# Down-projection weight loads issued by ScalarE on its own DMA queue, in a mixture-of-experts block

## The reference

```python
x = x + merged @ w_out[l]                       # attention and pooling, 256 x 1024
h2 = rms_norm(x, norm2_g[l])
x = x + moe_ffn(h2, router_w[l], ...)

def moe_ffn(...):                               # top 4 of 32 experts, softmax gates
    ...
    def run_block(args):
        tok, e = args
        xb = h_pad[tok]
        gu = xb @ w_gate_up[e] + b_gate_up[e]                  # 1024 x 2048
        gate = jnp.minimum(gu[:, :EXPERT_DIM], SWIGLU_LIMIT)
        up = jnp.clip(gu[:, EXPERT_DIM:], -SWIGLU_LIMIT, SWIGLU_LIMIT)
        act = gate * jax.nn.sigmoid(SWIGLU_ALPHA * gate) * (up + 1.0)
        return act @ w_down[e] + b_down[e]                     # 1024 x 1024
```

## Time and profile before

| | us |
|---|---|
| median of 3 runs | 1127.81 |
| lowest and highest | 1127.17, 1128.42 |
| the profiled execution | 1124.1 |
| its span | 1122.3 |

### The profile page before, as it was taken

How to read it: one execution, slowest core, us unless ns; L and a number is a source line. 1 busy time by engine, 2 the same in 40 slices (tenths; PEclk the granted TensorE clock), 3 DMA queues, 4 the chain that set the end, 5 groups by cost and what they waited for, 6 DMA issues and landing times.

```text
span 1122.3 us, 11997 instructions
## 1 busy us (share of the span) xinstructions
PE 1051.0 (94%) x4830; PEld 439.1 (39%) x4830; DVE 290.4 (26%) x592; ACT 118.0 (11%) x210; POOL 7.7 (1%) x16
## 2 busy tenths in 40 slices
PE   7999999999999999999999989898989899999988
PEld 4444545543434343434343424242424243333332
DVE  2654032332222222221212121221212212212221
ACT  3124101201000000000000000000000000000001
POOL 2000000000000000000000000000000000000000
PEclk9999999999999999999999999999999999999999
DMA  9932573899999999999999999999999999999995
GB/s 335 392 130 84 216 279 117 336 385 430 428 427 428 429 425 427 422 429 429 428 428 427 430 429 429 429 428 429 427 430 429 429 428 428 430 426 430 429 429 220
DMA packets 40256, 430.32 MB, mean 383 GB/s; under 512 B 5024, under 2 KB 5152, under 8 KB 15536
## 3 DMA queue, kind: packets, MB, share of 16 engines
q1 hardware_dynamic: 39280, 428.11, 91.4%
q0 software_dynamic: 672, 1.91, 0.5%
q10 hardware_dynamic: 288, 0.08, 0.0%
HBM read 429.03 MB, written 1.05 MB: 383 GB/s over the span
## 4 chain that ended last, share of the span: by engine, by line
PE 73%; DMA 22%; DVE 2%; issue 1%; ACT 0%; SPq 0%; DVEq 0%
PE bank L1194 28%; DMA slot<-w_gate_up_dram 18%; PE bank L1219 14%; PE bank L917 9%; PE bank L1139 5%; PE bank L1168 5%; DMA slot<-w_down_dram 4%; PE bank L941 4%; PE bank L1208 2%; DVE x L838 2%; PE bank L1117 1%; PE bank L892 1%; PE bank L1179 1%; DMA consts<-consts_dram 0%; PE bank L1235 0%
## 5 line engine op out<-in xcount | busy, mean ns | idle before, releaser
L1194 PE MATMUL bank<-slot,scr 128*64 128x512 f32 x2048 | 458.8, 596 | 20.5 <-DMA slot<-w_gate_up_dram 20.4
L1194 PEld LDWEIGHTS bank<-slot,scr 128*64 128x64 f32 x2048 | 142.3, 137 | 305.9 <-issue 268.6
L1219 PE MATMUL bank<-slot,scr 128*64 128x512 f32 x1008 | 229.1, 596 | 11.1 <-DMA slot<-w_down_dram 10.4
L813 DVE COPY scr<-bank 128x512 f32<-128x512 f32 x32 | 22.1, 691 | 456.6 <-PE bank L1194 456.6
L1219 PEld LDWEIGHTS bank<-slot,scr 128*64 128x64 f32 x1008 | 68.6, 137 | 144.9 <-issue 120.0
L917 PE MATMUL bank<-slot,scr 128*128 128x512 f32 (+1 forms) x256 | 103.3, 563 | 0.8 <-DVE scr L531 0.8
L1168 PE MATMUL bank<-scr 64*128 64x512 f32 x240 | 59.6, 613 | 22.0 <-DVE x L838 22.0
L838 DVE TENSOR_TENSOR x<-bank,x 128x512 f32<-128x512 f32 x64 | 41.4, 686 | 105.3 <-PE bank L1168 103.1
L819 DVE TENSOR_TENSOR scr<-bank,bgu 128x512 f32<-128x512 f32 x64 | 41.2, 686 | 104.9 <-PE bank L1208 104.9
L917 PEld LDWEIGHTS bank<-slot,scr 128*128 128x128 f32 x256 | 46.5, 194 | 53.7 <-issue 52.5
L1139 PEld LDWEIGHTS bank<-scr,xn 128*128 128x128 f32 x480 | 57.7, 196 | 12.2 <-issue 12.2
(11 more groups left out here) (184 smaller groups left out, 389.1 us busy)
## 6 DMA issues: line engine op xcount, KB each, us to landing
slot<-w_gate_up_dram SPq DMA_DIRECT2D x128, 2048.0 KB, 29.2
slot<-w_down_dram SPq DMA_DIRECT2D x63, 2048.0 KB, 20.9
slot<-w_in_dram SPq DMA_DIRECT2D x14, 1024.0 KB, 15.5
slot<-w_out_dram SPq DMA_DIRECT2D x4, 1024.0 KB, 4.9
slot<-w_branch_attn_dram SPq DMA_DIRECT2D x2, 1024.0 KB, 13.9
slot<-w_branch_pool_dram SPq DMA_DIRECT2D x2, 1024.0 KB, 8.5
slot<-w_down_dram SPq DMA_DIRECT2D x2, 1024.0 KB, 7.2
x<-x_dram SPq DMA_DIRECT2D x2, 512.0 KB, 5.7
```

What stands on the lines that cost most here:

```text
L813: V.tensor_copy(gu_sb[:, 512:1024], GB[1][:, :]).then_inc(gu_copied[1], 1)
L1194: ins = MM(GB[h][T * g:T * g + T, :], xgT[:, k, T * e:T * e + T], gu_slot[s][:, c0:c0 + 512], start=k == 0, stop=k == KC - 1)
L1219: ins = MM(DB[T * h:T * h + T, :], actT[e][:, c, :], v3(dn_slot[j][:, :], 4)[:, k, 512 * h:512 * h + 512], start=c == 0, stop=c == KC - 1)
```

## The change

SP's program loses the down loads of the loop and their waits (`downs_a`, `downs_b`). It issues gate/up loads alone, each as soon as its slot is used; the loops for the first pairs become one plain loop. The first two down loads (expert 0) and the last two (expert 31) stay on SP. ScalarE issues the others: after each `copy_d` it issues the two down units of the next expert, on its own queue. It needs no wait of its own for the slots, since `copy_d` waited for `dn_used[1]` and so for both halves. Sizes, slots and all other engines' programs are as before.

```diff
-            gates_a(2, 1)
-            gates_b(2, 1)
-            downs_b(0, 2)
-            for p in range(2, EARLY):
-                ahead = EARLY - p
-                gates_a(2 * p, p, 0, ahead)
-                downs_a(2 * p - 2, 2 * p - 1)
-                gates_a(2 * p, p, ahead, 4)
-                gates_b(2 * p, p, 0, ahead)
-                downs_b(2 * p - 2, 2 * p)
-                gates_b(2 * p, p, ahead, 4)
+            for p in range(1, EARLY):
+                gates_a(2 * p, p)
+                gates_b(2 * p, p)
...
-            downs_a(2 * EARLY - 2, 2 * EARLY - 1)
             with sp.Fori(EARLY - 1, n - 1) as it:
...
                 gates_a(here, q)
-                downs_b(sp.snap(2 * (it % PAIRS)), q2)
                 gates_b(here, q)
-                downs_a(here, q3)
...
+            def load_down(expert):
+                for j in range(DN_SLOTS):
+                    act.dma_start(dn_slot[j][:, :], dn_src(expert, j)).then_inc(dn_in[j], 16)
+
+            def pair(here, after, q, q1, q2, q3, last):
                 act.wait_ge(done["S"], q)
                 nc.scalar.activation(selgT, SB[:, :], ACT.Copy).then_inc(read["S"], 1)
                 copy_gu(1, q, q2)
                 sigmoid(q2)
                 copy_d(0, q2)
                 if not last:
+                    load_down(here + 1)
+                if not last:
                     copy_gu(0, q1, q3)
                     sigmoid(q3)
                     copy_d(1, q3)
+                    load_down(after)
```

More of the change, by code:

```diff
@@ L308, in gates_b @@
                     load_gu(4 + i, expert + 1)
[L310 to L318, removed]
-            gates_a(2, 1)
-            gates_b(2, 1)
-            downs_b(0, 2)
-            for p in range(2, EARLY):
-                ahead = EARLY - p
-                gates_a(2 * p, p, 0, ahead)
-                downs_a(2 * p - 2, 2 * p - 1)
-                gates_a(2 * p, p, ahead, 4)
-                gates_b(2 * p, p, 0, ahead)
-                downs_b(2 * p - 2, 2 * p)
-                gates_b(2 * p, p, ahead, 4)
+            for p in range(1, EARLY):
+                gates_a(2 * p, p)
+                gates_b(2 * p, p)
             sp.wait_ge(n_ready, 1)
             n = sp.value_load(n_t[0:1, 0:1], min_val=PAIRS, max_val=4 * PAIRS)
-            downs_a(2 * EARLY - 2, 2 * EARLY - 1)
             with sp.Fori(EARLY - 1, n - 1) as it:
-                here, q, q2, q3 = sp.snap(2 * ((it + 1) % PAIRS)), sp.snap(it + 1), sp.snap(2 * it + 2), sp.snap(2 * it + 3)
+                here, q = sp.snap(2 * ((it + 1) % PAIRS)), sp.snap(it + 1)
                 gates_a(here, q)
-                downs_b(sp.snap(2 * (it % PAIRS)), q2)
                 gates_b(here, q)
-                downs_a(here, q3)
             sp.wait_ge(dn_used[0], sp.snap(2 * n))
@@ L481, in copy_d @@
                 nc.scalar.activation(dsb[:, 512 * e:512 * e + 512], DB[:, :], ACT.Copy).then_inc(d_copied, 1)
-            def pair(q, q1, q2, q3, last):
+            def load_down(expert):
+                for j in range(DN_SLOTS):
+                    act.dma_start(dn_slot[j][:, :], dn_src(expert, j)).then_inc(dn_in[j], 16)
+            def pair(here, after, q, q1, q2, q3, last):
                 act.wait_ge(done["S"], q)
@@ L492, in pair @@
                     copy_d(1, q3)
+                    load_down(after)
             copy_gu(0, 1, 1)
             sigmoid(1)
-            pair(1, 2, 2, 3, False)
+            pair(0, 2, 1, 2, 2, 3, False)
             act.wait_ge(n_ready, 1)
@@ L499, in _ @@
             with act.Fori(1, n - 1) as it:
-                pair(act.snap(it + 1), act.snap(it + 2), act.snap(2 * it + 2), act.snap(2 * it + 3), False)
-            pair(n, None, act.snap(2 * n), act.snap(2 * n + 1), True)
+                pair(act.snap(2 * (it % PAIRS)), act.snap(2 * ((it + 1) % PAIRS)), act.snap(it + 1), act.snap(it + 2), act.snap(2 * it + 2), act.snap(2 * it + 3), False)
+            pair(None, None, n, None, act.snap(2 * n), act.snap(2 * n + 1), True)
             act.wait_ge(d_done, act.snap(2 * n + 1))
```

## The result

| | before | after |
|---|---|---|
| median, us | 1127.17 | 1146.03 |
| lowest and highest | 1123.89, 1128.42 | 1145.82, 1151.41 |
| runs | 5 | 5 |
| profiled execution | 1124.1 | 1146.0 |
| its span | 1122.3 | 1144.2 |

The changed kernel takes 1.0182 times as long (95% interval 1.0162 to 1.0202), 18.9 us by the medians. The forecast was 1151.1, with 1137 to 1160 as its range. The profiled executions lie 21.9 us apart; the forecast for that pair was 23.3.

The account below looks back on a forecast made before the run. DMA engines bound the late stage (58.7 us a pair, PE 54.2). A new 4.7 us PE stall was to hold early pairs at 58.8 too: +23.3 us in sum, 1147.4 profiled, 1151.1 median, range 1137 to 1160.

Parts of the forecast that it names:

- The two stages: Kernel before: early pairs of experts at PE's 54.2 us, spending the stock of full slots; late pairs at DMA's 58.7.
- The gain of SP's freedom: SP's gate/up loads no longer wait for down slots (714.0 us of waits): worth nothing while DMA engines are never idle.
- The gap at 255 us: At the first even expert's down product, DMA engines stand idle 2.9 us before the first down unit begins.
- Issue: ScalarE issues the down units after its copy; the first leaves 0.7 us after the down product's end.
- Landing beside a full queue: After even products, down units land 12 and 22 us from issue, with 1.0 us of fixed time put in front.
- The half share: While SP's and ScalarE's queues both have work, each gets half the rate; two down units take 19.56 us.
- The stall and its shape: PE waits 4.7 us in each pair for the second down unit, at the odd expert's second down half.
- (b): Rival: one order by issue; down units wait behind SP's backlog g, stall g - 5.8 us, 1145 us; chance 0.09.
- (a): Rival: transfers alternate whole; pairs of 56.5 us, then +2.9 idle and +8.2 at the end, 1139 us; chance 0.13.
- (c): Rival: two queues cost DMA rate; 1% gives pairs of 59.3 us and 1158, 2% gives 1165; chance 0.08.
- (d): Rival: not slower; ScalarE's queue gets clearly more than half, and both queues together exceed 429 GB/s; chance 0.12.
- The median: Profiled execution forecast at 1147.4 us; 3.7 added, as before it lay under the timed median: 1151.1.

Follow-up runs that it names:

- sp_holds: The changed kernel, but SP keeps its waits for dn_used at their old places and issues nothing there, so gate/up loads don't run ahead: 1187.95 us, 1.0527.
- packets8_after: The changed kernel with gate/up loads cut into packets of 8 KB instead of 16 KB, down packets staying at 16 KB: 1146.04 us, 1.0182.
- release_order: The kernel before, all loads on SP's queue, but issued in the order in which slots come free: 1144.17 us, 1.0153.
- early_first: The changed kernel, but ScalarE issues the first down unit ahead of its sigmoid, after the down product's first half, the second after the second half: 1133.91 us, 1.0050.
- filler_four: The changed kernel with four idle matmuls ahead of the odd expert's second down half in pairs 2 to 13: 1153.70 us, 1.0231.

## Why the prediction was right

**The two stages** were read rightly, and what became of them too: no pair of 54.2 from pair 2 to pair 13, a mean of 58.87 (13 pairs, 276.89 to 1042.18: 765.3 us; the sum had 764.4), then 54.20 in pair 15, as worked out. Pair 16 starts at 1096.38; the sum had 1097.2. The last of the thirteen, pair 14, already took 54.4, and the twelve ahead of it 59.24 in the mean; over these the DMA share is 1.01 at 428 GB/s. So what held the mean near 58.8 was the pace of the DMA engines, which was the bound in the prediction too, and not a stall of the forecast size in every pair. The gain of SP's freedom was costed at nothing for the pace, and the DMA share shows none. But to put this term at nothing was wrong: sp_holds, without it, is 42 us slower, since PE's pair then lies above the DMA pace.

**The gap at 255 us** is there, and the engines are idle at the end. Busy times (last: granted clock, DMA share, GB/s):

```profile
250.00:260.00 10.00, 10.00 (x50) 3.99 (x52) 3.44 (x6) 1.23 (x2) 0.00 (x0) 1.00 0.76 283
1080.00:1100.00 20.00, 20.00 (x98) 7.12 (x96) 5.39 (x11) 1.82 (x3) 0.00 (x0) 1.00 0.66 262
```

2.4 us of ten are idle in the first, 2.9 forecast; 1.01 stood there before. In bytes the loss is larger, 283 GB/s for 431, or 3.4 us of transfer. From 1080 to 1100 us the share is 0.66, from 1100 to 1120 0.41: the full slots that are worth nothing at the end.

**Issue.** I had the loads 0.7 us behind the product's end. They leave with the copy, not behind it. ScalarE in order of time:

```profile
254.75 0.60 ACT L460 ACTIVATE scr<-bank 128x512 f32<-128x512 f32 x1 [1.58 <-PE bank L1205]
254.75 0.82 ACTq L464 DMA_DIRECT2D slot<-w_down_dram  x2
```

ScalarE's queue issues while its copy runs (the timeline above merges the two loads into 0.82 us from the copy's start): in the loop at 309.44, 0.2 us behind the product's end. The first stall (pair 1) was 0.2 us and not 1.7: the unit landed at 273.19, wanted at 251.11 + 3.61 + 18.32 = 273.04. Some 0.7 of the 1.5 us are the earlier issue; the rest I can't place.

**Landing beside a full queue** was the term that decides, and it was a little short. ScalarE's two loads of pair 2, from issue to landing (us):

```profile
DMA to landing us min/median/max: 14.7/19.3/24.0
```

12.5 and 22.3 us were worked out, 14.7 and 24.0 measured. The half share itself holds, within a few per cent. The DMA queues, 314 to 330 us (packets, MB, share):

```profile
q10 hardware_dynamic: 238, 3.64, 53.5%
q1 hardware_dynamic: 225, 3.18, 46.7%
```

The term that was short is the one in front. This is all that moves from 309.6 to 312.8 us, behind the issue at 309.44:

```profile
q1 hardware_dynamic: 101, 1.39, 102.3%
```

The first packet of ScalarE's queue starts only near 312.9, 3.4 us behind the issue, where 1.0 had been put; for the load with nothing in front packets run within 1 us. The data of both units then take 18.3 us (19.6 forecast), and the end 2.7 (1.7). So beside a full queue there is a start of over 3 us ahead of the half share, here and in packets8_after. The first unit lands 1.3 us too late by it; the prediction had it fine by 0.5.

**The stall and its shape** were wrong in size, though not in sum. I had 4.7 us in every pair. Pair 2 has 6.4 and a lower clock behind it, together 8.6; from pair 5 to 12 short and long pairs alternate, 55.1 to 55.7 and 61 to 62.7 us. The reason that the prediction gave for taking 58.8 (where SP's queue runs empty, the down units get the full rate) is the one at work, only harder: PE, at over 60 us, falls behind the DMA engines, SP's queue drains (pair 5 above), the next pair has a stall of 0.9 to 1.4 us only. sp_holds, where the held loads fill the queue in each window, keeps over 61 in each pair. The lower clock behind a stall had no term in the sum.

**Rivals.** (b) gave 1145 for one queue, and release_order measured 1144.2; in the changed kernel itself it is out by the share. By its own terms its stall is g - 5.1 us (0.7 + 2.7 + g + 9.8 - 18.3), not g - 5.8, which moves its 1145 by under 1 us. (a) as a whole didn't come, since pairs weren't of 56.5 us; its end was seen in packets8_after. (c) is out: from pair 2 to pair 13 the rate is 428 GB/s, as in the kernel before. (d) is out, and early_first shows how near its first half comes: 5.9 us from the kernel before.

**The median** was missed by 5 us, 1.4 of them by the sum. The rest is that I carried over the 3.7 us by which the profiled execution of the kernel before lay under its median; the profiled execution of the changed kernel lies on its median. Single executions of either kernel differ by 4 to 6 us, and the last section shows one place where such a difference can come from.

## What to carry to other kernels

Moving loads to a second queue changes when they land, not how fast the engines run: beside a full queue they get a share that follows the packet sizes, so a unit that took 7.6 us with nothing in front took 14.7, and the second of two 24.0. Work out issue-to-need against that, from the first instruction that can release the buffer, and ask what the loads now overtake at the end.

Where transfers are the bound in the late stage only, look at what PE gains in the early one: a stall that hides within the late pace can still cost the whole stock that was built up. And with all loads in one queue, an order of consumption was worth more than never waiting: the order alone cost 17 us here. Beside a second queue it was the other way: there SP's running ahead was worth 42.

## What the runs showed of the hardware

A PE that stood for some 5 us went on at half its clock (1.2 instead of 2.4 GHz) for some microseconds. In the stretch around the stall of pair 2 the mean granted clock is 0.66 (busy times, then clock, DMA share, GB/s):

```profile
330.00:340.00 10.00, 6.02 (x20) 1.84 (x22) 3.45 (x9) 0.88 (x2) 0.00 (x0) 0.66 1.00 425
```

Sixteen down matmuls took 5.72 us there and 3.65 after stalls of 0.9 to 1.4 us. In between both are seen: 3.65 behind the 2.5 us of packets8_after, but 5.35 behind a stall of 2.4 us in pair 3 of the changed kernel (its chain):

```profile
392.70 5.35 PE bank L1205 x16
```

So the length of a stall alone doesn't say what follows. In this kernel no cost of it was seen, because the DMA pace stood behind it (filler_four), but in sp_holds it was 2.9 us of the pair shown.

The clock also differs where the kernels don't. From 97 to 102 us, in the attention part, no load is under way and the programs are alike, yet the profile of the changed kernel has 1.00 (first) and that of release_order 0.66 (second; columns: stretch, busy times, clock, DMA share, GB/s):

```profile
97.00:102.00 5.00, 5.00 (x14) 2.13 (x13) 3.89 (x5) 2.56 (x11) 0.00 (x0) 1.00 0.00 0
```

release_order:

```profile
97.00:102.00 5.00, 5.00 (x9) 2.18 (x9) 4.61 (x6) 2.55 (x13) 0.00 (x0) 0.66 0.00 0
```

In that profile pair 2 starts at 280.68, in the other at 276.89. So two profiles may differ by 4 us ahead of anything that was changed; a difference of a few us is best read from a common point on.

The engines alternate between a hardware queue of SP and one of ScalarE, as they did between SP's and GpSimd's: with 16 KB packets on one and 8 KB on the other 189 to 190 in ten us, 2.83 to 1.44 MB. The Trainium skill (DMA: Bandwidth & Descriptors, Queues, rings and completion order) puts the turn at packets of some 9 to 17 descriptors. If such a turn took in all that a load gives one engine, the 8 KB loads would have kept half of the bytes; the count doesn't agree with that. It fits turns of single records, or of an equal number of records from each queue.
